# The sample outer product of the scan fused with its addition on VectorE

## The reference

```
c_new = w_old[..., None, None] * c + jnp.einsum('bsh,bshd,bshv->bhdv', w_s, kc, vc)
num   = att ... + w_inter[..., None] * jnp.einsum('bthd,bhdv->bthv', qc, c)
```

## Time and profile before

| | us |
|---|---|
| three runs | 3469.32 (median), 3462.81, 3485.54 |
| the profiled execution | 3478.18 |
| its span, first to last instruction | 3476.2 |
| DVE busy over the span | 2539.1 (73%) |
| ACT busy | 949.7 (27%) |
| PE busy | 3147.4 (91%) |
| POOL busy | 1715.6 (49%) |

### The profile page before, as it was taken

One profiled execution on the slowest core, in us unless ns is written; L12 is line 12 of the kernel. 1 busy time (PEld: TensorE's weight loads), 2 busy tenths in 40 slices (PEclk: granted clock), 3 DMA queues, 4 the chain that ended last, 5 costly groups with the idle time before them and its releaser, 6 DMA issues.

```text
span 3476.2 us, 42684 instructions
## 1 busy us (share of the span) xinstructions
PE 3147.4 (91%) x13863; PEld 2080.1 (60%) x13863; DVE 2539.1 (73%) x5317; ACT 949.7 (27%) x2199; POOL 1715.6 (49%) x1420
## 2 busy tenths in 40 slices
PE   8989999999788888888868667999999999999998
PEld 8987887877433233333334445776667766677764
DVE  6672000799487888888889996777777777777777
ACT  3112222566111111211158781111111111111111
POOL 3341221344024666667654555555555555555553
PEclk9999999999899999999989898999999999999999
DMA  4324433778757999999999999999999999999996
GB/s 148 88 68 161 154 146 120 245 273 310 276 169 281 347 364 356 368 362 365 353 340 329 346 351 388 387 393 383 385 399 394 376 383 371 390 398 389 388 380 241
DMA packets 385327, 1074.38 MB, mean 309 GB/s; under 512 B 55128, under 2 KB 145144, under 8 KB 378848
## 3 DMA queue, kind: packets, MB, share of 16 engines
q0 software_dynamic: 186624, 679.56, 51.9%
q1 hardware_dynamic: 146592, 308.65, 24.7%
q10 hardware_dynamic: 51904, 83.63, 6.5%
HBM read 978.52 MB, written 93.05 MB: 308 GB/s over the span
## 4 chain that ended last, share of the span: by engine, by line
PE 38%; DVE 14%; DMA 10%; issue 7%; POOL 3%; ACT 1%; another core or an unknown queue 0%; DVEq 0%; POOLq 0%; SPq 0%; ACTq 0%
PE PB L2184 16%; PE PB L2171 13%; DVE ub L1840 5%; DMA x1d<-in_peer_u 4%; DMA vbf<-in_peer_v,gixv 3%; PE PB L2160 3%; PE PB L2147 2%; PE PB L2211 2%; DMA ub<-in_peer_u,gix 2%; POOL vbf L1570 1%; DVE ohb L1787 1%; POOL ub L1570 1%; DVE oha L1785 1%; PE PB L2129 1%; DVE work L1670 1%
## 5 line engine op out<-in xcount | busy, mean ns | idle before, releaser
L1570 POOL DMA_INDIRECT ub<-in_peer_u,gix x640 | 696.4, 1088 | 738.3 <-DVE hid L1840 522.2
L2184 PE MATMUL PB<-vbd,wd 128*128 128x512 f32 x1536 | 684.8, 596 | 0.0
L2171 PE MATMUL PB<-xds,uts 128*128 128x384 f32 x3072 | 569.6, 340 | 0.0
L2171 PEld LDWEIGHTS PB<-xds,uts 128*128 128x128 f32 x3072 | 531.8, 189 | 0.5 <-issue 0.5
L1570 POOL DMA_INDIRECT vbf<-in_peer_v,gix x340 | 392.5, 1154 | 166.0 <-issue 100.6
L2184 PEld LDWEIGHTS PB<-vbd,wd 128*128 128x128 f32 x1536 | 283.8, 191 | 309.6 <-issue 309.6
L2211 PE MATMUL PB<-vbf,dg 128*64 128x512 f32 x1200 | 326.8, 669 | 112.2 <-DMA vbf<-in_peer_v,gixv 91.1
L1570 POOL DMA_INDIRECT vbf<-in_peer_v,gixv x300 | 319.7, 1066 | 179.4 <-issue 84.9
L1801 DVE TENSOR_TENSOR uts<-PB,uts 128x512 fp32r<-128x512 f32 x256 | 175.7, 686 | 304.1 <-ACT uts L2017 291.3
L1840 DVE CUSTOM_DVE_ANT_0 ub<-ub,x1g 128x1024 f32<-128x1024 f32 x257 | 312.7, 1221 | 51.7 <-DMA ub<-in_peer_u,gix 39.1
L2017 ACT CAST uts<-PB 128x512 fp32r<-128x512 f32 x256 | 150.1, 586 | 646.1 <-PE PB L2160 610.1
(11 more groups left out here) (397 smaller groups left out, 5220.7 us busy)
## 6 DMA issues: line engine op xcount, KB each, us to landing
vbd<-in_peer_v SPq DMA_DIRECT2D x128, 512.0 KB
x1d<-in_peer_u SPq DMA_DIRECT2D x96, 512.0 KB
gd_d<-stag ACTq DMA_DIRECT2D x12, 2048.0 KB
gbd<-gd_d SPq DMA_DIRECT2D x16, 1536.0 KB
ubd<-in_peer_u SPq DMA_DIRECT2D x32, 512.0 KB
wtr<-in_w_tok SPq DMA_DIRECT2D x6, 2048.0 KB, 8.5
tok_d<-stg ACTq DMA_DIRECT2D x48, 256.0 KB, 2.0
rb_e<-rows_d SPq DMA_DIRECT2D x8, 1536.0 KB, 9.6
```

The costliest lines, as they stand in the source:

```text
L1570: pool.indirect_dma_start(out=buf, out_offset=None, in_=a[table], in_offset=bass.IndirectOffsetOnAxis(ap=index, axis=0)).then_inc(done, 16)
L2171: last = T.matmul(PB[:, 6, 0:TD], uts[:, b % 2, ul, k, :], xds[:, xl, k, :], start=(k, n) == (0, 0), stop=(k, n) == (KD - 1, 2))
L2184: last = T.matmul(PB[:, 2 * d + n, :], wd[:, b % 2, d * CH:(d + 1) * CH], vbd[b % 8][:, n * 512:(n + 1) * 512], start=b == 0, stop=b == NB ...
```

## The change

ScalarE no longer writes the outer product to `t4`; it keeps the decay of `cs`. VectorE's addition of 2048 elements becomes eight operations of 256 elements, each of which reads the value row and one block of `cs`, multiplies the value by the scalar of each partition, adds, and writes the block back. The signal `outer` becomes `decayed`. ScalarE's wait for `c_new` of the sample before goes, as there is no `t4` to protect (it was already met through `sample_out`). SP's first late load of `wo` now waits for seven `c_new` in place of seven `outer`, as it is now VectorE that reads `vb0` last. The tile `t4` is replaced by one of the same size that nobody uses, so that all addresses stay.

```diff
-    t3, t4 = sb("t3s", [P, 8, NST]), sb("t4s", [P, MH * KT, DK])
+    t3 = sb("t3s", [P, 8, NST])
+    sb("outer_gap", [P, MH * KT * DK])
...
-            sp.wait_ge(ss["outer"], NCH - 1)
+            sp.wait_ge(ss["c_new"], NCH - 1)
             late_w_out(1)
...
                 if i:
                     sample_out(i - 1)
-                free(act, ss["c_new"], i)
                 for h in range(MH):
...
-                    S.activation(cs[q][:, 2 * h:2 * h + 2, :], cs[q][:, 2 * h:2 * h + 2, :], ACT.Copy, scale=scl[:, 8 + h, i:i + 1])
-                    for k in range(KT):
-                        j = h * KT + k
-                        last = S.activation(t4[:, j, :], vb[q][:, h * DK:(h + 1) * DK], ACT.Copy, scale=scl[:, 12 + j, i:i + 1])
-                last.then_inc(ss["outer"], 1)
+                    last = S.activation(cs[q][:, 2 * h:2 * h + 2, :], cs[q][:, 2 * h:2 * h + 2, :], ACT.Copy, scale=scl[:, 8 + h, i:i + 1])
+                last.then_inc(ss["decayed"], 1)
...
             def sample_end(n):
-                dve.wait_ge(ss["outer"], n + 1)
-                V.tensor_tensor(cs[n % 2][:, :, :], cs[n % 2][:, :, :], t4[:, :, :], ALU.add).then_inc(ss["c_new"], 1)
+                dve.wait_ge(ss["decayed"], n + 1)
+                for j in range(MH * KT):
+                    h = j // KT
+                    last = V.scalar_tensor_tensor(cs[n % 2][:, j, :], vb[n % 2][:, h * DK:(h + 1) * DK], scl[:, 12 + j, n:n + 1], cs[n % 2][:, j, :], ALU.mult, ALU.add)
+                last.then_inc(ss["c_new"], 1)
```

More of the change, by code:

```diff
@@ L634, in build_scan @@
     ss = {n: sem("smp_" + n) for n in (
-        "ld zo bct bcc bcd qk qkc exp arg nst cur decay outer st_new red c_new summed num numc num_out num_in den end").split()}
+        "ld zo bct bcc bcd qk qkc exp arg nst cur decay decayed st_new red c_new summed num numc num_out num_in den end").split()}
     s_in = [sem(f"smp_states_loaded{q}") for q in range(2)]
```

## The result

The changed kernel takes 3493.69 us (median of 12 runs, 3489.78 to 3500.30) against 3466.51 for the kernel before in the same comparison (12 runs, 3458.24 to 3485.54). The ratio is 1.0068, with an interval from 1.0053 to 1.0083: 23.6 us slower, 18 to 29. (The two medians by themselves are 27.2 us apart.) The forecast was 18.9 us slower.

What follows compares the result with a forecast made beforehand. VectorE's (DVE's) list was taken to bound the scan loop; 18.0 us from the seven iterations plus 0.95 for the last sample gave + 18.9, 3488 us from the median. The range was 3469 to 3503 us.

Steps and rivals of the forecast that it cites:

- the prediction's own signs: Checks in the changed kernel's profile: usual iterations 35.9 us, loop clock 1.00, last L824 at 885.30 + 19, PEER within 6 us.
- the second case: On DVE and POOL, L1110 goes ahead of `hT`: + 9.3 us, time 3479, chance 0.30.
- What bounds the loop: In the scan, DVE's list is the loop: its added work is paid, ACT's lost work gains 0.
- The train: Eight fused DVE operations replacing L1107: 0.394 us each, 3.15 in all, 5.31 with `og` inside.
- the half rate: Rival on DVE's fused operations: two steps per element, 0.66 us each; + 36 us, time 3506, chance 0.03.
- the case without exclusion: Rival on DVE and POOL: fused operations don't wait for `og`; 0 us, time 3469, chance 0.04.
- `hT` ahead of L1110: POOL's `hT` asks 0.13 us before L1110 and goes first; L1146 2.33 us later in six iterations, 4.03 in one.
- first rival: L1110 beats `hT`: L1146 starts at t + 9.41, 0.95 us more in six iterations; + 9.3 us, chance 0.30.
- My rule that one already asked for gets its turn at the next end: DVE operations with two SBUF inputs and POOL's run one after the other; edge between POOL 0.03 late and 0.14 late.
- the rival that had it: TensorE's clock falls in the loop, 3.5 us in each of seven iterations: + 25 on top of 18.9, time 3513, chance 0.05.
- the only such stretch: End of the scan, where PE had been idle 4 to 5 us and its clock fell; the loop's forecast gap was 3.6.
- The end of the scan: Last sample's train + 0.95 us, paid in full; SP's later `wo` loads hidden by PE's `wo` products, 0 taken, up to 3.

Runs made afterwards that it cites:

- the ACT experiment: Changed kernel with ScalarE still writing the outer product to the old tile `t4`, where nobody reads it: 3466.23 us, ratio 1.0053 to the kernel before.
- the timed-again kernel: The changed kernel, unaltered, timed a second time beside the kernel before: 3476.34 us, ratio 1.0082.
- those with added products: Changed kernel with five or three unused matmuls added on PE in its gap before L1146's result: 3461.88 us, ratio 1.0033 (five); 3457.27 us, ratio 1.0028 (three).
- the variants with a shorter last iteration: Changed kernel with `og` behind `hT`, six or seven fused operations, ACT's writes, or added products: last iteration 23.0 to 26.9 us; ratios 0.9987 to 1.0053.
- seven operations: Changed kernel with seven of the eight fused operations, the last block of each sample's state left as decayed: 3480.41 us, ratio 1.0015.
- the addition in eight parts: Kernel before with its one addition L1107 cut into eight tensor_tensor of 256, ScalarE still writing the outer product: 3451.70 us, ratio 1.0013.
- the kernel before with the exchange: Kernel before with GpSimd's `og` issued behind its `hT` instead of ahead of it: 3441.02 us, ratio 0.9965.

## Why the prediction was right, and where it was off

The time is inside the range, 3493.7 for 3488, or 23.6 us of difference for 18.9. The number is better than the account behind it: a term of 10 us, more than half of the forecast, was taken as nothing, and the number stayed near because a part of it was made up by a collision that came less often than forecast, and the rest is small beside a range of 34 us. By the prediction's own signs the account of the iteration fails: it said that iterations over 37 us would refute it, and the long ones are 37.4 to 37.6; it asked for a clock of 1.00 in all windows of the loop; and PE's last L825 started 25.8 us later than L824 before, counted from the first train, not 19. (The PEER phase, its other sign, is 2.1 us shorter in the first pair of profiles, within the 6 allowed. Between profiles of different chips it varies by up to 41 us, so it was no good sign. And the range's lower end doesn't follow as written: the second case, 3479, less 6 is 3473, not 3469.) By its steps:

**What bounds the loop: right, but not all of it.** DVE's list, and 25 us less on ACT brought nothing, by the ACT experiment too. But where the clock fell DVE waits 1.33 us for PE's products before `num`, so in those iterations PE is on the path as well.

**The train: right.** Forecast 0.394 for one of eight, measured 0.395 to 0.396, and `og` inside the train in nearly all iterations: L1110 issued at t + 5.27, forecast 5.31. (In one of the seven iterations of the timed-again kernel `og` asked while the eighth operation ran and was served behind L1110, and that one took 32.89 us.)

**The rivals on the operation's price: excluded.** By the Trainium skill, page "VectorE: DVE Perf Modes", section "The TRN2 errata", I had estimated 2.6 us for a train that nothing holds up; the trace has 3.16 to 3.17 and doesn't agree. Nor does it with the half rate of the Trainium skill, page "Vector Engine (DVE) Microarchitecture Reference", section "Points that are easy to get wrong", which by my estimate would have made it 5.3. And POOL's `og` and the fused operations took turns, as forecast: the case without exclusion is out.

**`hT` ahead of L1110: right in size, not in all.** Where it is, L1146 starts at t + 10.74 (forecast 10.79). Where it is not, at 9.37 (the first rival's 9.41). The forecast had it in all seven iterations of the loop; it was in five of seven, then three, then five. Forecast and first rival were put as two cases, and the kernel is a mixture of them. The lead that I worked out as 0.13 us is 0.08 to 0.12 as recorded, and it doesn't decide. In the six profiles with this train (the changed kernel's three, those with added products, and that with ACT's writes) `hT` was first 22 times, with leads of 0.083 to 0.098 us, and L1110 was first 16 times, with `hT` 0.085 to 0.117 ahead. Even a larger lead could lose. This is the iteration of 32.89 us, which starts at 645.24:

```profile
648.28 3.57 POOL L1072 TENSOR_TENSOR og<-zo,gm 128x1024 f32<-128x1024 f32 x1 [3.51 <-DMA zo<-tok_d]
648.41 1.22 DVE L1110 TENSOR_TENSOR t3s<-st,bb 128x1024 f32<-128x1024 f32 x1
```

`og` asked 0.14 us ahead and L1110 took its bare 1.22. So it went in all four iterations of these profiles in which `og` asked 0.14 to 0.21 us ahead of L1110, while behind the single L1107 leads of 0.17 and 0.21 won. My rule that one already asked for gets its turn at the next end, with an edge somewhere below 0.14 us, can't be applied to recorded starts so close together. The two iterations in which L1110 was first took 2 x 1.4 us from the forecast.

**The clock: the term that was mis-sized.** The forecast had it at 0 and full clock in all windows; the rival that had it gave 3.5 us in each of seven iterations and a chance of 0.05. It fell in six of seven and cost 1.67 in each, 10 us. The gap was forecast well (3.6, measured 3.55). The failed step is the argument "the gap of 3.6 is shorter than the 4 to 5 us that PE had been idle in the only such stretch": one stretch where the clock fell says nothing of how short a gap may be. The price failed too. PE is at half clock for 3.4 us and not 7, and half of that, 1.7, is what it costs. And the rival was set up as a case of its own with a small chance, when the fall comes with the forecast's own long wait in each iteration where `hT` wins, 16 of 16 in the three profiles of the changed kernel and that with ACT's writes.

**The end of the scan: right by luck in part.** The last train is +0.95 as forecast; the whole stretch took 37.6, 36.5 and 37.7 us in the three profiles of the changed kernel, for 36.1 and 36.8 before. The rest was not followed. The delay of SP's loads was taken at 0 with 3 us as the other bound. Alone it costs 4.4. In the changed kernel it is hidden, not by the row that I named (PE's list of `wo` products waits for it) but, as the variants with a shorter last iteration suggest, by the long last iteration.

**Ratio and sum.** 24.9 + 1.5 in the scan of the profile, 18 to 29 in the ratio. The forecast's 18.0 + 0.95 and this differ by: clock +10.0, `hT` -2.8, the rest -0.3 and +0.6. The sum of the profile, 26.4, is 3 us above the ratio's 23.6 and inside its interval.

Not settled: why the first phase ends at 645 or 657 us; what decides between `hT` and L1110 at recorded leads of 0.08 to 0.12 us; and why the clock also fell in 4 of 11 iterations in which L1110 was first and PE had waited some 2.17 us (same four profiles) and in one of seven with seven operations, but in none of the seven with the addition in eight parts, with the same wait.

## What to carry to other kernels

When a list of VectorE operations grows, write down when each GpSimd operation on SBUF asks, and see which of them the list's new end passes: that, not the added work, was three quarters of the cost here. Putting the GpSimd operation beside VectorE's operations that read PSUM was worth 9 to 11 us of loop, while taking work off an engine that waits gave nothing. And a longer wait of TensorE costs more than its length when its products behind the wait are themselves on the path; a trace where the clock holds at one length of wait doesn't say that it holds at twice that.

## What the runs showed of the hardware

- TensorE's granted clock fell to 1.2 GHz after a wait of 3.55 us in every such iteration (16 of 16), and after 2.17 us in 5 of 25, and was back at 2.4 GHz 3.4 us after it had fallen. In the loop of the kernel before, the usual wait of 1.7 us never did it. Filling 2.6 us of the 3.55 with products that nobody reads kept 2.4 GHz, and made the kernel faster.
- An operation of VectorE with two inputs in SBUF and one of GpSimd exclude each other for a train of small operations as for a large one: `og` got its turn between two of the eight, and held the train up by 2.1 to 2.2 us, for scalar_tensor_tensor and for tensor_tensor. L1146, which reads PSUM, took its usual 1.22 us beside `hT` (the kernel before with the exchange, at 757.54).
- Recorded starts within some 0.2 us of each other don't tell which of the two is first: with GpSimd's `hT` 0.083 to 0.098 us ahead it was first 22 times, and with it 0.085 to 0.117 ahead VectorE was first 16 times.
- 256 elements cost 0.395 us fused and 0.335 as an addition, the step from one to the next.
